# One SBUF tensor cut in three, and sixteen more columns in another: a two-block transformer forward pass on one core

## What is computed

```python
def first_block(x, c, ...):
    for l in range(2):
        mod = silu(c) @ mod_w[l] + mod_b[l]
        sh_m, sc_m, g_m, sh_f, sc_f, g_f = split(mod, 6)
        h = rms_norm(x, norm_g[l, 0]) * (1 + sc_m) + sh_m
        y = conformer_conv(h, ...) if l == 0 else diff_attention(h, k_shared, v_shared, ...)
        x = x + g_m * rms_norm(y, norm_g[l, 1])
        h = rms_norm(x, norm_g[l, 2]) * (1 + sc_f) + sh_f
        x = x + g_f * rms_norm(conv_ffn(h, ...), norm_g[l, 3])

def second_block(x, ...):
    z = rmsnorm(x, g) @ w_in
    y_a, y_b = dsa_sparse_attention(...), mla_attention(...)
    x = x + (gate0 * (y_a @ w_branch_a) + gate1 * (y_b @ w_branch_b)) @ w_out
    x = x + square(relu(rmsnorm(x, g2) @ w_ff1)) @ w_ff2
    return rmsnorm(x, final_g)
```

## Time and profile before

| | |
|---|---|
| median of 3 runs | 2182.34 us (2177.34 to 2184.02) |
| the profiled execution, its own time | 2182.34 us |
| its span, first to last instruction | 2180.5 us |
| TensorE (PE) busy | 2080.8 us, 95% of the span |
| VectorE (DVE), ScalarE (ACT), GpSimd (POOL) busy | 1343.5, 869.6, 156.4 us |
| mean granted TensorE clock | 0.98 of full speed |
| moved by DMA | 225 MB, mean 103 GB/s |

### The profile page before, as it was taken

One profiled execution on the slowest core, in us unless ns is written; L12 is line 12 of the kernel. 1 busy time (PEld: TensorE's weight loads), 2 busy tenths in 40 slices (PEclk: granted clock), 3 DMA queues, 4 the chain that ended last, 5 costly groups with the idle time before them and its releaser, 6 DMA issues.

```text
span 2180.5 us, 26178 instructions
## 1 busy us (share of the span) xinstructions
PE 2080.8 (95%) x10575; PEld 1660.1 (76%) x10575; DVE 1343.5 (62%) x2282; ACT 869.6 (40%) x1454; POOL 156.4 (7%) x105
## 2 busy tenths in 40 slices
PE   5999999999999999899999999999888999999998
PEld 4755868888887886676888887788666788888886
DVE  7698468856844556647775566547876565624532
ACT  3455534423433245534442343333266533422421
POOL 0464100000010000020000000000000000000000
PEclk9999999999999999999999999999999999999999
DMA  8343225665531220012233323222213122333331
GB/s 300 128 149 111 72 72 187 201 202 184 179 101 59 70 86 30 30 58 64 97 100 115 101 92 102 73 84 81 63 44 114 52 83 91 97 97 96 97 97 68
DMA packets 67112, 225.01 MB, mean 103 GB/s; under 512 B 7216, under 2 KB 8112, under 8 KB 66992
## 3 DMA queue, kind: packets, MB, share of 16 engines
q1 hardware_dynamic: 64112, 218.11, 31.0%
q10 hardware_dynamic: 2880, 5.24, 0.7%
HBM read 215.98 MB, written 7.34 MB: 102 GB/s over the span
## 4 chain that ended last, share of the span: by engine, by line
PE 82%; DVE 10%; ACT 4%; issue 3%; DMA 0%; POOL 0%; SPq 0%; DVEq 0%; POOLq 0%; ACTq 0%
PE bank L288 23%; PE bank L290 22%; PE bank L289 22%; PE bank L293 14%; DVE wlo L328 1%; ACT whi L315 1%; DVE sc L2083 1%; PE bank L815 1%; DVE steps L2081 1%; ACT pr L788 1%; DVE pr L780 0%; DVE tmp L544 0%; DVE Hl L549 0%; ACT sc L788 0%; POOL small L524 0%
## 5 line engine op out<-in xcount | busy, mean ns | idle before, releaser
L288 PE MATMUL bank<-Hh,whi 128*128 128x512 f32 x1632 | 655.7, 402 | 25.2 <-DVE wlo L328 9.9
L290 PE MATMUL bank<-Hh,wlo 128*128 128x512 f32 x1632 | 641.5, 393 | 0.0
L289 PE MATMUL bank<-Hl,whi 128*128 128x512 f32 x1632 | 640.7, 393 | 0.0
L328 DVE TENSOR_TENSOR wlo<-stg,whi 128x1024 fp32r<-128x1024 f32 (+1 forms) x299 | 358.8, 1205 | 419.3 <-ACT whi L315 418.7
L315 ACT ACTIVATE whi<-stg 128x1024 fp32r<-128x1024 f32 (+1 forms) x309 | 312.9, 1025 | 416.9 <-PE bank L290 408.9
L288 PEld LDWEIGHTS bank<-Hh,whi 128*128 128x128 f32 x1632 | 310.0, 190 | 95.9 <-DVE wlo L328 11.5
L290 PEld LDWEIGHTS bank<-Hh,wlo 128*128 128x128 f32 x1632 | 309.1, 189 | 65.9
L289 PEld LDWEIGHTS bank<-Hl,whi 128*128 128x128 f32 x1632 | 310.1, 190 | 62.1 <-issue 1.5
L288 PE MATMUL bank<-HIDh,whi 128*128 128x512 f32 x352 | 141.6, 402 | 0.0
L289 PE MATMUL bank<-HIDl,whi 128*128 128x512 f32 x352 | 138.0, 392 | 0.0
L290 PE MATMUL bank<-HIDh,wlo 128*128 128x512 f32 x352 | 138.0, 392 | 0.0
(11 more groups left out here) (294 smaller groups left out, 2765.3 us busy)
## 6 DMA issues: line engine op xcount, KB each, us to landing
raw<-in_mod_w SPq DMA_DIRECT2D x96, 512.0 KB, 4.2
stg<-in_ffn_in SPq DMA_DIRECT2D x88, 512.0 KB, 3.8
stg<-in_ff SPq DMA_DIRECT2D x64, 512.0 KB, 3.5
stg<-in_ffn_out SPq DMA_DIRECT2D x40, 512.0 KB, 3.6
stg<-in_cm_w SPq DMA_DIRECT2D x24, 512.0 KB, 3.6
stg<-in_gates SPq DMA_DIRECT2D x16, 512.0 KB, 3.5
stg<-in_z_ch SPq DMA_DIRECT2D x12, 512.0 KB, 3.5
bias_kept<-out_b ACTq DMA_DIRECT2D x20, 256.0 KB, 2.1
```

The source lines that it names most:

```text
L288: pe.e.matmul(out_, l[0], r[0], start=start, stop=False, skip_group_check=True)
L289: pe.e.matmul(out_, l[0], r[1], start=False, stop=False, skip_group_check=True)
L290: return pe.e.matmul(out_, l[1], r[0], start=False, stop=stop, skip_group_check=True)
L328: hand.e.tensor_tensor(wlo[j % NW][:, 0:n * c], stg[j % NSTG][:, 0:n * c], whi[j % NW][:, 0:n * c].bitcast(F32), ALU.subtract).then_inc(*m ...
```

## The change

The tensor `columns` of 1357 float32 columns is replaced by three tensors `vec`, `cst` and `tab` with the same contents, and `small` gets 96 columns in place of 80. No other line is changed.

```diff
-        columns = sb("columns", [P, NV + C_N + 40 + 256])
-        vec, cst, tab = columns[:, 0:NV], columns[:, NV:NV + C_N], columns[:, NV + C_N:]
+        vec = sb("vec", [P, NV])
+        cst = sb("cst", [P, C_N])
+        tab = sb("tab", [P, 40 + 256])
         ones, ident = sb("ones", [P, P]), sb("ident", [P, P])
         causal = sb("causal", [P, S])
-        small = sb("small", [P, 80])
+        small = sb("small", [P, 96])
```

## The result

The changed kernel has a median of 2197.59 us (2194.15 to 2199.85, 6 runs), the kernel before 2179.59 us (2177.34 to 2184.02, 6 runs). The ratio is 1.0069, 95% interval 1.0056 to 1.0083: slower by 15 us (12 to 18). The medians of six are 18 us apart; all 17 runs of the changed kernel on record have a median of 2195.18 us. Part of the gap goes with the mean granted clock of TensorE, 0.979 on average in those 17 runs and 0.981 in the 44 of the kernel before that were taken beside the experiments. Among runs with the same mean clock the gap is 11 to 12 us (at 0.980, means of 2194.6 and 2183.1 us). Why the slower kernel was granted a little less is not shown.

The account below looks back on a forecast made before the run. TensorE, busy 95% of 2180.5 us, was taken to bound the kernel through its pace of matmuls. Terms of 0 for VectorE, ScalarE, TensorE and DMA, and 0 to 0.3 us for GpSimd, gave 2182.3 us, range 2175 to 2190.

Parts of the forecast that it names:

- The list of what moves: SBUF places: nearly all tensors behind `small` move by 96 bytes; no instruction, wait, DMA or moved byte is added or removed.
- VectorE, ScalarE, GpSimd at 0 to 0.3 us: Element-wise work on moved tensors: no price for VectorE and ScalarE, 0 to 0.3 us for GpSimd's powers and sums.
- DMA at 0: Transfers filling `raw` and `c_act` and reading `out_b` at new positions: taken as 0, up to 2.3 us.
- TensorE at 0, up to 14.7: 2076 three-product matmuls on moved HID, MG and CQ tensors, now 32 bytes off: taken as 0, at most 14.7 us.
- The bound of that term: Moved three-product matmuls: 471 us / 32 = 14.7 us, if rows were fed in 64-byte pieces, 33 in place of 32.
- rival 1: Fast matmuls on moved tensors pay for starting 32 bytes off: 2197.0 us, +0.7%, chance 0.04.
- The line of 16 bytes: SBUF read in 16-byte lines: shifts of 32 or 96 bytes keep operands' places within lines, so TensorE's term would be 0.
- The range: Whole kernel: 2175 to 2190 us, the no-change band and a little on both sides, with rivals 1 and 2 beyond.

## Why the prediction was wrong

- *The list of what moves*, by 96 bytes behind `small`, and that no instruction, wait or transfer changes: right. The move behind `small` alone made the difference, as the kernel with the cut and without that move (ratio 1.0003) shows.
- *VectorE, ScalarE, GpSimd at 0 to 0.3 us*: right, the medians above are within 1 ns, the two powers at the same 1.03 and 1.02 us.
- *DMA at 0*: no sign of more. TensorE's added 12.1 us account for the profile's 12.2. The median of `raw` to landing went from 4.2 to 4.4 us, but it is 4.4 as well in the kernel with everything moved, which lost no time (ratio 1.0003).
- *TensorE at 0, up to 14.7*: this is the step that failed. I took 0 because the convolution's rows show no such step. The rows were read rightly: fp32 matmuls stay at 429 ns at every distance tried. But they were of the other kind, and in the trace of before every fp32r matmul on these tensors had distance 0 modulo 256, the one place where there is no cost. That sample could not speak for other distances. The kernels of matmuls alone then measured 226.7 ns at 0 and 233.4 at 96.
- *The bound of that term* was nearly its size: 12.2 us by the distances in the trace (2076 x 6.7 ns would be 13.9, but layer 1 was not at 226.7 before, and some of the 2076 stand before a wait or a burst), 15 us (12 to 18) by the ratio, against 14.7. Its mechanism (33 pieces of 64 bytes in place of 32) was wrong: a start at a multiple of 64 still cost 1.0031, and a start 32 off cost nothing when the weights were 32 off too. That the two numbers are near is chance. The sign that the prediction gave for rival 1, `HID` and `MG` at 0.23 us while `Hh` stays, did appear, but it cannot tell a cost of the start from a cost of the distance.
- *The line of 16 bytes* from the Trainium skill ("SBUF — State Buffer", note on cachelines) gave 0 here, and the runs gave +6.7 ns a matmul for a shift by 96, a multiple of 16. The same page of the Trainium skill, in its section "Who interferes with whom", calls the read ports for moving rows and for weights independent. The runs show that where they lie relative to one another matters all the same: 226.7, 233.4 with the weights alone moved by 32, 226.7 with both.
- *The range* left out a bound of an unknown cost, 2197.0, on the strength of a chance of 0.04. The sum itself said that the trace did not show this kind of matmul off its place, and such a bound belongs inside.

What stays open: what passes between the two streams, why one distance costs more than another, and why one load of weights 100 off cost nothing among others at 0. It is shown that the distance modulo 256 sets the pace where all matmuls of a stream have the same one, and that a weight load acts on the matmul beside it; how the reads collide is not.

## What to carry to other kernels

A padding or a cut of one small tensor moves all tensors behind it, and with them the distance between moved rows and weights; in a kernel bound by fp32r matmuls of 512 columns, keep it at 0 modulo 256 bytes (here 227 ns a matmul, otherwise 228 to 240), and check it after each change of the allocation. The mark in a profile is a pace of matmuls that changes for some tensors only, while idle times and all other engines stay. When a term of a forecast rests on rows of another kind of instruction, keep its bound in the range.

## What the runs showed of the hardware that I had not expected

- fp32r matmuls of 512 columns: 226.7 ns at distance 0, up to 240.0, repeating every 256 bytes. With 256 columns 0 is not the best: 120.0 ns at 0, 113.3 at 112. With 128 columns 111.6 to 111.7 at all five distances tried. fp32: 429.2 to 429.5 a record, two records a matmul. bf16: 215.8 to 216.4 at the five distances tried.
- One matmul out of place slows others behind it that are in place: with its row 100 off, six distances, its own and five behind it, take 228 to 236 ns in place of 227. After a burst of 24 bf16 matmuls of 32 columns, the next six distances of fp32r matmuls at distance 0 average 232 ns.
- A record can be missing from a trace: a distance of twice the pace, with weight loads that go on in step, is a gap in the records and not a slow matmul.
